# Biases of the experts added in PSUM, down weights in 8 KB runs and a rebuilt end, in a block of mixer and experts

## What is computed

```python
logits = (xt @ w_router + b_router)
top_vals, top_idx = lax.top_k(logits, TOP_K)          # 4 of 32
gates = jax.nn.softmax(top_vals, axis=-1)
...
gu = xblk @ w_gu[e] + b_gu[e]                          # 1024 -> 2048
x_glu = jnp.minimum(gu[:, :F], SWIGLU_LIMIT)           # 7.0
x_lin = jnp.clip(gu[:, F:], -SWIGLU_LIMIT, SWIGLU_LIMIT)
act = x_glu * jax.nn.sigmoid(SWIGLU_ALPHA * x_glu) * (x_lin + 1.0)
return act @ w_down[e] + b_down[e]                     # 1024 -> 1024
...
return rms_norm(x, norm_final_w)
```

## Time and profile before

| what | us |
|---|---|
| median of 3 executions | 1301.28 (1299.1 to 1305.61) |
| the profiled execution, its own time | 1300.23 |
| its span, first to last instruction | 1298.4 |
| VectorE busy in the span | 1138.5 |
| TensorE busy (products) | 1153.1 |
| ScalarE busy | 930.8 |
| time in GpSimd's instructions | 527.2 |

### The profile page before, as it was taken

The page is one execution under the profiler, slowest core; times in us unless marked ns, Lnnn a source line. Parts: engine busy times, 40 slices in busy tenths (PEclk is TensorE's granted clock), DMA queues, the critical chain, the costliest instruction groups (busy, mean ns, idle before and its releaser), DMA issues.

```text
span 1298.4 us, 38721 instructions
## 1 busy us (share of the span) xinstructions
PE 1153.1 (89%) x16938; PEld 873.6 (67%) x16939; DVE 1138.5 (88%) x868; ACT 930.8 (72%) x817; POOL 527.2 (41%) x69
## 2 busy tenths in 40 slices
PE   5999998789999899998998899989999899898975
PEld 2455544777777777776777677767777677677752
DVE  5742454789999999999999999999999999999995
ACT  5332423578888888888788888888888888888872
POOL 0120300006666666661664066406644165363521
PEclk9999999899999999999999999999999999999998
DMA  9502231799999999999999999999999999999974
GB/s 347 213 31 100 84 127 65 281 375 373 403 406 406 405 405 406 406 405 406 397 406 406 396 399 405 407 396 396 406 406 406 395 397 406 406 396 407 399 288 143
DMA packets 87315, 444.93 MB, mean 343 GB/s; under 512 B 8896, under 2 KB 9408, under 8 KB 54272
## 3 DMA queue, kind: packets, MB, share of 16 engines
q1 hardware_dynamic: 82400, 427.99, 81.6%
q0 software_dynamic: 3472, 12.19, 4.8%
q10 hardware_dynamic: 1296, 2.44, 0.6%
HBM read 426.21 MB, written 16.38 MB: 341 GB/s over the span
## 4 chain that ended last, share of the span: by engine, by line
DVE 35%; issue 25%; PE 18%; DMA 16%; ACT 4%; DVEq 1%; SPq 0%; ACTq 0%
DVE ring L390 24%; DMA ring<-in_w_down_dram 8%; PE ps L1060 8%; PE ps L1162 4%; DMA ring<-in_w_gu_dram 4%; DMA arena<-in_w_down_dram 4%; DVE arena L465 3%; ACT ring L387 3%; PE ps L411 2%; DVE arena L486 1%; DVE arena L477 1%; DVE arena L471 1%; DVE arena L480 1%; PE ps L438 1%; DVE arena L474 1%
## 5 line engine op out<-in xcount | busy, mean ns | idle before, releaser
L460 POOL DMA_INDIRECT acc<-arena,slot_row x31 | 502.2, 16199 | 614.7 <-ACT arena L493 614.7
L390 DVE SCALAR_TENSOR_TENSOR ring<-ring 128x2048 f16<-128x2048 f32 x290 | 654.0, 2279 | 25.6 <-ACT ring L387 25.4
L387 ACT ACTIVATE ring<-ring 128x2048 f16<-128x2048 f32 x290 | 549.5, 1906 | 119.9 <-DMA ring<-in_w_gu_dram 66.1
L411 PE MATMUL ps<-arena,ring 128*128 128x88 f16 x12288 | 521.8, 205 | 89.6 <-DVE ring L390 73.8
L411 PEld LDWEIGHTS ps<-arena,ring 128*128 128x128 f16 x12288 | 492.9, 100 | 122.0 <-DVE ring L390 72.6
L438 PE MATMUL ps<-ring,arena 128*88 128x512 f16 x1536 | 340.7, 381 | 11.0 <-DVE ring L390 4.4
L438 PEld LDWEIGHTS ps<-ring,arena 128*88 128x88 f16 x1536 | 181.6, 120 | 156.9 <-DVE ring L390 8.2
L390 DVE SCALAR_TENSOR_TENSOR ring<-arena,ring 128x2048 f16<-128x2048 f32 x94 | 212.5, 2279 | 2.2 <-ACT ring L387 2.0
L387 ACT ACTIVATE ring<-arena 128x2048 f16<-128x2048 f32 x94 | 178.7, 1905 | 27.0 <-DMA arena<-in_w_down_dram 17.7
L404 PE MATMUL ps<-arena 128*128 128x88 f16 x2048 | 92.6, 206 | 6.7 <-issue 3.4
L404 PEld LDWEIGHTS ps<-arena 128*128 128x128 f16 x2048 | 85.6, 101 | 7.4 <-issue 7.1
(11 more groups left out here) (135 smaller groups left out, 531.0 us busy)
## 6 DMA issues: line engine op xcount, KB each, us to landing
ring<-in_w_gu_dram SPq DMA_DIRECT2D x194, 1024.0 KB, 15.4
ring<-in_w_down_dram SPq DMA_DIRECT2D x96, 1024.0 KB, 15.1
arena<-in_w_gu_dram SPq DMA_DIRECT2D x62, 1024.0 KB
arena<-in_w_down_dram SPq DMA_DIRECT2D x32, 1024.0 KB
ring<-in_w_in_dram SPq DMA_DIRECT2D x4, 2048.0 KB, 12.5
ring<-in_w_out_dram SPq DMA_DIRECT2D x2, 2048.0 KB, 8.5
arena<-in_x_dram SPq DMA_DIRECT2D x4, 512.0 KB, 12.2
ring<-in_w_in_dram SPq DMA_DIRECT2D x2, 1024.0 KB, 11.5
```

The source lines that it names most:

```text
L387: return act.activation(split_of(slot)[:, 0, :], raw(r), ACT.Copy, scale=SCALE_W)
L390: return dve.scalar_tensor_tensor(split_of(slot)[:, 1, :], raw(r), SCALE_W, split_of(slot)[:, 0, :], ALU.mult, ALU.subtract)
L411: mm = pe.matmul(o, w[:, i, col:col + P], src[:, j, k, :], start=start and n == 0, stop=stop and n == 2, skip_group_check=True)
L460: return pool.indirect_dma_start(out=acc, out_offset=bass.IndirectOffsetOnAxis(ap=rows, axis=0), in_=y_row[0:SCAT, :], in_offset=None, com ...
```

## The change

The gate-up biases are no longer turned. They are loaded as 2 x 32 rows of 2048, split in a high and a low float16 part by ScalarE and VectorE before the last residual, and for each expert 16 products with a one-hot column of that expert (`own`, scaled) start the sums in PSUM with the bias. So the bias step of VectorE goes; the clamps read PSUM, one with the scale, and the scale of the other moves into the next steps. The down weights come with two neighbouring rows on each partition, 8 KB in one run; for the features to match, the gate-up products take every other column of the weight as their 128 columns. The end: on the last expert the steps on VectorE and ScalarE stand in another order, the table for the root is loaded ahead, and the test for further blocks is turned round, so that the last part of the program stands in both of its branches, with the usual one first.

```diff
         def load_dn(sp, j, e, slot):
-            src = w_down[0, bass.ds(e, 1), 2 * j * P:2 * (j + 1) * P, :].rearrange("a (j p) c -> p (a j) c", p=P)
-            return sp.dma_start(raw(slot).rearrange("p (j c) -> p j c", j=2), src)
+            src = w_down[0, bass.ds(e, 1), 2 * j * P:2 * (j + 1) * P, :].rearrange("a (p i) c -> (a p) (i c)", i=2)
+            return sp.dma_start(raw(slot), src)
...
-        def gu_tile(b, j):
-            return 2 * b + j if j < 2 else NF // 2 + 2 * b + j - 2
+        def every_other(first):
+            return slice(first, first + 2 * P - 1, 2)
+
+        def gu_cols(b, j):
+            return every_other(F * (j // 2) + 2 * b * P + j % 2)
+
+        def pe_bias(pe, e):
+            for b in range(GB):
+                for j in range(PER):
+                    pe.matmul(GU[:, b, j * CAP:(j + 1) * CAP], bgu_parts[:, gu_cols(b, j)],
+                              own[:, bass.ds(e, 1)].to_broadcast([P, CAP]), start=(j == 0), stop=False,
+                              skip_group_check=True)
 
         def pe_gu(pe, slot, q, k, b):
             for j in range(PER):
-                f = gu_tile(b, j)
-                mm = product(pe, GU[:, b, j * CAP:(j + 1) * CAP], split_of(slot), f * P, xT[:, q], k,
-                             k == 0 and j == 0, k == KD - 1)
+                mm = product(pe, GU[:, b, j * CAP:(j + 1) * CAP], split_of(slot), gu_cols(b, j), xT[:, q], k,
+                             False, k == KD - 1)
...
-        def dve_bias(dve, e):
-            return dve.scalar_tensor_tensor(
-                gub.rearrange("p b h (j c) -> p b (h j) c", j=2), GU.rearrange("p b (j c) -> p b j c", j=PER), UNSCALE,
-                bguT[:, bass.ds(e, 1), :].rearrange("p a (b j) -> p (a b) j", b=GB).unsqueeze(3)
-                .to_broadcast([P, GB, PER, CAP]), ALU.mult, ALU.add)
+        LIM = LIMIT / UNSCALE
 
         def dve_glu(dve):
-            return dve.tensor_scalar(gub[:, :, 0], gub[:, :, 0], LIMIT, None, ALU.min)
+            return dve.tensor_scalar(gub[:, :, 0], GU[:, :, 0:2 * CAP], LIM, UNSCALE, ALU.min, ALU.mult)
 
         def dve_lin(dve):
-            return dve.tensor_scalar(gub[:, :, 1], gub[:, :, 1], LIMIT, -LIMIT, ALU.min, ALU.max)
+            return dve.tensor_scalar(gub[:, :, 1], GU[:, :, 2 * CAP:4 * CAP], LIM, -LIM, ALU.min, ALU.max)
...
-        def further_blocks(eng, block, skip_block, setup=None):
-
-
-            most = eng.value_load(count_max_i[0:1, 0:1], min_val=0, max_val=S)
-            with eng.If(most > CAP):
+        def ending(eng, most, rest, block, skip_block, setup=None):
+
+
+            with eng.If(most <= CAP):
+                rest()
+            with eng.Else():
...
+                rest()
...
             early(0)
             early(1)
+            sp.wait_ge(mix_turned, H)
+            for i in range(2):
+                sp.dma_start(bgu_raw[32 * i:32 * i + E, :], b_gu[0]).then_inc(bgu_loaded, 16)
...
-            act.dma_start(bgu_raw[:, :], b_gu[0].rearrange("e (q c) -> (e q) c", q=4)).then_inc(bgu_loaded, 16)
...
+                if t == 1:
+                    act.wait_ge(bgu_loaded, 32)
+                    act.activation(bgu_parts[0:64, :], bgu_raw, ACT.Copy, scale=SCALE_W).then_inc(bgu_high, 1)
...
             high(E // 2, 0, 0)
-            high(E // 2, 0, 1)
             finish_rows(E - 2, nth(E, 0))
             act_high_part(E - 1)
+            high(E // 2, 0, 1)
...
+            act.activation(std[:, 15, 0:1], eps_t[:, :], ACT.Sqrt).then_inc(root_table, 1)
...
             turn_qk(1)
-            turn_bgu()
...
             def stage(s, q, last=False, more_meta=True):
+                pe.wait_ge(gu_taken, s)
+                pe_bias(pe, s)
                 pe.wait_ge(xT_ready, 2 * s + 2)
-                pe.wait_ge(gu_taken, s)
...
+                if t == NT - 1:
+                    dve.memset(late[64:P, :], 0.0)
+                    dve.wait_ge(bgu_high, 1)
+                    dve.scalar_tensor_tensor(bgu_parts[32:64, :], bgu_raw[32:64, :], SCALE_W, bgu_parts[32:64, :],
+                                             ALU.mult, ALU.subtract).then_inc(bgu_ready, 1)
                 residual(t)
...
-                dve_bias(dve, e).then_inc(gu_taken, 1)
-
-            def clamped(e):
-                dve.wait_ge(gu_taken, e + 1)
                 dve_glu(dve).then_inc(glu_ready, 1)
-                dve_lin(dve).then_inc(lin_ready, 1)
+                dve_lin(dve).then_inc(gu_taken, 1)
...
                     low(h, q, 10)
-                    biased(s, nth(s, GU_CH))
+                    taken(s, nth(s, GU_CH))
                     low(h, q, 11)
-                    clamped(s)
...
             multiplied(E - 1)
+            activated(E - 1)
             low(E // 2, 0, 0)
-            activated(E - 1)
+            act_low_part(E - 1)
             low(E // 2, 0, 1)
-            act_low_part(E - 1)
```

More of the change, by code:

```diff
@@ L200, in build_program @@
         turned = [("x", t, i) for t in range(NT) for i in range(2)]
[L201 removed]
+        turned += [("qk", n) for n in range(2)] + [("qk", n) for n in range(2, 8)]
         turned += [("s", h, i) for h in range(H) for i in range(NT)]
@@ L315, in build_program @@
         scattered = sem("scattered")
-        more = {k: sem(f"more_{k}") for k in ("high", "low", "used", "onehot", "gathered", "xT", "biased",
+        more = {k: sem(f"more_{k}") for k in ("high", "low", "used", "onehot", "gathered", "xT",
                                               "glu", "lin", "prod", "sig", "act32", "ah", "act",
@@ L1013, in skip, with rest @@
                 act.sem_inc(more["xT"], 2)
-            further_blocks(act, one, skip, last_added)
-            for t in range(NT):
-                act.wait_ge(acc_ready, 2 * t + 2)
-                act.activation(o_row[:, t, :], x_sb[:, t, :], ACT.Square, accum_out=ss[:, 12 + t, 0:1])\
-                    .then_inc(ss_ready, 1)
-                root(1, D)
+            def rest():
+                norms[0] = 12
+                for t in range(NT):
+                    act.wait_ge(acc_ready, 2 * t + 2)
+                    act.activation(o_row[:, t, :], x_sb[:, t, :], ACT.Square, accum_out=ss[:, 12 + t, 0:1])\
+                        .then_inc(ss_ready, 1)
+                    root(1, D)
+            ending(act, most, rest, one, skip, last_added)
         @block.tensor
@@ L1027, in _ @@
             pe.wait_ge(small_loaded, 16)
-            def turn_bgu():
-                pe.wait_ge(bgu_loaded, 16)
-                for j in range(4):
-                    take(pe, ("bgu", j))
-                    pe.transpose(bank(("bgu", j))[:, 0:P], bgu_raw[:, j * P:(j + 1) * P], ident).then_inc(bgu_turned, 1)
             def turn_x(t):
@@ L1264, in _ @@
             gather(1, 0)
+            pe.wait_ge(gu_taken, 1)
+            pe_bias(pe, 1)
             pe.wait_ge(xT_ready, 4)
-            pe.wait_ge(gu_taken, 1)
             for k in range(7):
@@ L1290, in _ @@
             mm.then_inc(wg_turned, 1)
+            most = most_slots(pe)
             pe.wait_ge(row_ready, 2 * E - 2)
             pe.wait_ge(act_ready, E)
-            down(E, 0, 0)
-            down(E, 1, 1)
-            down(E, 2, 2)
-            down(E, 3, 3)
-            pe.wait_ge(counts_ready, 1)
+            for j in range(DN_CH):
+                down(E, j, j)
             def last_added():
@@ L1328, in skip, with rest @@
                 pe.sem_inc(more["used"], CH)
-            further_blocks(pe, one, skip, last_added)
-            pe.wait_ge(wgT_ready, 1)
-            pe.wait_ge(tail_loaded, 32)
-            pe.wait_ge(row_ready, 2 * E)
-            for m in range(2 * NT):
-                t, half = m // 2, m % 2
-                pe.matmul(ps[:, m, :], wgT[:, t * P:(t + 1) * P], y_last[:, half * 512:(half + 1) * 512],
-                          start=True, stop=True).then_inc(bias_done, 1)
+            def rest():
+                pe.wait_ge(wgT_ready, 1)
+                pe.wait_ge(tail_loaded, 32)
+                pe.wait_ge(row_ready, 2 * E)
+                for m in range(2 * NT):
+                    t, half = m // 2, m % 2
+                    pe.matmul(ps[:, m, :], wgT[:, t * P:(t + 1) * P], y_last[:, half * 512:(half + 1) * 512],
+                              start=True, stop=True).then_inc(bias_done, 1)
+            ending(pe, most, rest, one, skip, last_added)
         @block.vector
@@ L1587, in gates_and_meta, with taken @@
                 dve.sem_inc(routed, 1)
-            def biased(e, done, first=False):
+            def taken(e, done, first=False):
                 dve.wait_ge(chunk_used, done)
@@ L1653, in _ @@
             low(0, 1, 2)
-            biased(0, GU_CH, first=True)
+            taken(0, GU_CH, first=True)
             low(0, 1, 3)
-            clamped(0)
             low(0, 1, 4)
```

131 lines of the change are left out of this document (66 added, 65 removed).

## The result

The changed kernel took 1289.09 us in the median (1288.06 to 1291.0, 4 runs), the kernel before beside it 1302.84 (1299.1 to 1305.61, 4 runs): ratio 0.9898, 95% interval 0.9868 to 0.9928, or 13.3 us less (9.4 to 17.2). Measured once more, beside the kernel before on chip 2, it took 1288.85 for 1300.81: ratio 0.9903 (0.9883 to 0.9923). The forecast was 13.3 us less. The sum was right; the experiments show that two of its terms were not, and that their errors came close to cancelling is luck.

What follows compares the result with a forecast made beforehand. The DMA engines were taken to bound the expert stream, VectorE close behind. Front -1.4, stream -9 (-3 runs, -6 VectorE's room) and end -2.9 summed to -13.3 us: 1288.0 us, range 1278 to 1299.

Steps and rivals of the forecast that it cites:

- The bound: Expert stage: the DMA engines need 32.21 us an expert, above VectorE's 31.67; TensorE, at 29.4, is third.
- Bias and clamps: VectorE, each expert: bias step out, two PSUM clamps of 0.884 us in; saves 0.8 us, period 30.9; TensorE's bias products free.
- 8 KB runs: Down loads at 418 in place of 414 GB/s: 0.10 us an expert, 3 us in 31; bounds 0 and 0.4 an expert.
- What is lost between the two: Expert stream: some 10 us went into late chunks VectorE couldn't make up; its new room regains 6 us, bounds 0 and 11.
- Front: Before the experts: four bias transposes go (-1.0 us) and early bias loads move; -1.4 us, bounds -2 and 0.
- End: After the last expert: earlier last low part (-1.8 us) and root table loaded early (-1.1); -2.9 us, bounds -5 and +1.
- SP's jump at the very end: Program end: with the short path next in line, SP's jump may cost 0 to 2 us after the last store.
- The first: Rival: the stream doesn't gain, the 10 us were lost inside the DMA engines; only front and end, 1297 us; chance 0.12.
- The second: Rival: the lost 10 us come back whole and down loads gain 0.3 us an expert; 1278 us; chance 0.08.
- third: Rival: the step of two slows gate-up weight loads to 61 ns, TensorE becomes the bound; 1499 us; chance 0.09.
- load spacing: Sign: TensorE's gate-up starts stay 39 ns apart; above 44 ns the forecast would be wrong.
- the turns of q and k: Sign in the front: the q and k turns come 0.43 us before each run of products.

Runs made afterwards that it cites:

- Biases alone: Kernel before with only the bias products on TensorE, no VectorE bias step and no bias transposes, 4 KB runs and old end: 1299.84 us, ratio 1.0001.
- runs alone: Kernel before with only the down weights in 8 KB runs and the matching step of two in the gate-up and bias columns: 1294.19 us, ratio 0.9935.
- 88 rows: Changed kernel adding each expert's rows to memory as 88 rows, not 96: 1286.98 us, ratio 0.9900; once more 1287.05, ratio 0.9899.

## Why the prediction was right, step by step

**The bound.** It named the DMA engines, with a need of 32.21 us an expert, and that they set the stream is borne out: taking away the added rows gave 34.5 us, giving VectorE room gave none. But then it treated VectorE, 99% busy in the earlier trace rows, as half a bound, and that fell.

**Bias and clamps.** Sizes right: 0.89 us for 0.884, a period of 30.86 for 30.9. The 16 bias products are free, even doubled.

**8 KB runs, -3 us: mis-sized.** It measured -8.5 (6.5 to 10.3) in the times and -6.5 in the traces' streams. The step that failed is "the gate-up loads are the row for this form already". The 414 GB/s of the down loads in 4 KB runs was read rightly from the earlier trace rows. But in 8 KB runs, in the same stretches, they moved at 422 to 426 GB/s, above the 418 that the gate-up loads reach in both kernels: 0.24 us an expert where 0.10 was put down. Why gate-up loads, which have pieces of 8 KB too, stay at 418 was not tried. The bound of 0.4 us an expert held. The Trainium skill (DMA: Bandwidth & Descriptors, Why small descriptors are slow) gave an estimate of 1.1%, which seemed to confirm the 1% between 414 and 418; the runs showed about twice that (2.4% in the windows, 0.21 of 10.13 us in the streams), and its advice to join only pieces of at most 256 B would have left this gain where it lay.

**What is lost between the two, -6 us: wrong.** The premise was that experts 2 to 31 should have taken 924 us on the DMA engines' need, took 934.56, and that VectorE's lack of room lost the 10 us. The step that failed is this cause. Biases alone gained nothing (1.2 us less to 1.6 more) though VectorE's floor fell by 0.81, and an extra step took the room away again at no cost that can be measured. The gap itself stayed. With the down loads at 424 GB/s the same sum is 20.07 + 9.89 + 2.01 = 31.97 us an expert, and 29 x 31.97 - 10 = 917 us; from the third to the last step runs alone took 927.09 and the changed kernel 929.16. So 10 to 12 us over the sum remain, with VectorE's room and without it. Whether they are lost somewhere or the sum is too low (the scatter's 2.01, the 418, the lead of 10) stays open.

So two errors nearly cancelled: 3 us put down for the runs where it was 6.5 to 8.5, and 6 for VectorE's room where it was 0 to 1.5. That the total came out at the forecast's 13.3 is luck in this part.

**Front, -1.4: -0.9.** In the mixer the two runs of products now start 5.6 us apart where it was 6.64 (TensorE's timeline of the changed kernel, start us, us):

```profile
39.50 5.34 PE L1076 MATMUL ps<-ring,arena 128*128 128x512 f16 x24
...
45.12 5.34 PE L1076 MATMUL ps<-ring,arena 128*128 128x512 f16 x24
```

The second one starts 1.56 us earlier than in the earlier trace rows, and so does the store ahead of the experts (232.33 for 233.89). At the first expert's step 0.9 of this is left. Whether it is the added bias products there that take the rest was not tried.

**End, -2.9: in the profiled executions -2.1, in the times -3.8 (2.3 to 5.2).** The rows that answer to the earlier trace rows:

```profile
1254.84 0.78 ACT L491 ACTIVATE arena<-arena 128x704 f16<-128x704 f32 x1
...
1255.65 0.97 DVE L494 TENSOR_TENSOR arena<-arena 128x704 f16<-128x704 f32 x1 [1.30 <-ACT arena L491]
...
1256.72 12.21 PE L450 MATMUL ps<-ring,arena 128*88 128x512 f16 x48 [2.64 <-DVE arena L494]
...
1270.12 1.28 ACT L996 ACT_TABLE_LOAD   x1
```

The low part (L494) now follows its input (1254.84 + 0.78 = 1255.62) at once; before it came 1.11 us behind (1264.35 for 1263.24). The 48 products start 12.39 us behind the last expert's step, before 13.80: -1.4 where 1.8 was forecast. The table load ends at 1271.40, ahead of the first square (1272.97), and from the first of the 16 last products to the start of the last output step there are 14.17 us (1270.25 to 1284.42) where it was 15.24 (1278.87 to 1294.11): -1.1, as forecast. SP's jump at the very end, 0 to 2 in the forecast, is small: from the last output step (1284.42) to the span's end 4.7 us, before 4.3. The new end was shorter than the old one in all traces that add every row: 43.6 to 45.3 us in nine, 46.0 to 48.2 in three. The means are 2.3 us apart, the lower end of the interval from the times.

**The rivals.** The first ("the stream doesn't gain, the 10 us were lost inside the DMA engines") was right that VectorE didn't lose the 10 us, and missed what the runs save; that the DMA engines lost them is not shown. The second and third are refuted. Of the signs named, period, clamp, load spacing, the turns of q and k 0.44 us before each run and the missing table load came true; 32.0 us from expert to expert were 32.23, and two down-only stretches of the changed kernel (325 to 332 and 357 to 364 us) ran at 425 and 424 GB/s and not 418.

## What to carry to other kernels

Here an engine that was 99% busy beside a queue that landed later and later was not a second bound: giving it room, or taking it away, changed nothing that could be measured until the DMA's load was cut. The landing times told the two cases apart (8.1 and 8.7 us with VectorE as the bound, 15.8 with the DMA engines), the DMA share did not, at 1.00 to 1.02 in either. When a transfer gets a new form, measure that transfer in that form in a short run: the row of another transfer with the same form gave less than half of the gain. And time that remains between a sum and a measurement has no cause until an edit has taken the supposed cause away.

## What was not expected of the hardware

- The down loads of 1 MB moved at 414 GB/s in 4 KB pieces and at 424 in 8 KB pieces in the same stretches, which is 2% of their time in the stream (0.21 of some 10 us), while both kinds kept the DMA share at 1.01 to 1.03. The gate-up loads, in 8 KB pieces too, ran at 418 beside both.
- With VectorE's floor under the DMA engines' need, the experts of the changed kernel do not settle at an even 32.2 us; they alternate between 30.86 and 33.7. GpSimd's issue of the added rows alternates with them, as its timeline in the changed kernel shows:

```profile
678.06 20.16 POOL L472 DMA_INDIRECT acc<-arena,slot_row  x1 [29.81 <-ACT arena L501]
711.11 1.71 POOL L472 DMA_INDIRECT acc<-arena,slot_row  x1 [12.89 <-ACT arena L501]
742.62 20.16 POOL L472 DMA_INDIRECT acc<-arena,slot_row  x1 [29.80 <-ACT arena L501]
```

  The same instruction takes 1.71 or 20.16 us, and the scatter is the likely partner of the cycle (without it there is none; with 88 rows the cycle is mostly three experts long). But in runs alone it takes 17.0 to 21.3 us each time from 600 to 760 us, and the periods are uneven there too (31.67 to 34.49). Which of the two drives the other was not tried.
- Adding 31 x 96 rows of 4 KB, 12.19 of 445.27 MB, decides who the bound is: without them the kernel is 34.5 us shorter.
